# Latent attention layer: keys two heads at a time, queries split into rotary and plain tiles, caches laid out by the host

## The chip, the core and the metric

The kernel runs on one core of a Trainium2 chip. The metric is the device time of one execution in microseconds (us). The engines are named as in the profile: PE is TensorE, DVE is VectorE, ACT is ScalarE, POOL is GpSimd, SP is SyncE, which only issues the loads of the weights.

## What is computed

One step of a four-layer streaming encoder with a model width of 1024, for 256 frames of a new stream and 64 frames of a running stream. The kernel carries both as T = 320 columns. Layers 0 and 3 mix tokens by sparse attention, layer 1 by a recurrence, layer 2 by latent attention; each is followed by a gated feed-forward part. Only layer 2's mixer is touched. It is, cut to what matters:

```python
cq, ckv, kpe = jnp.split(h @ w_in, [512, 768], axis=-1)
q = (_rmsnorm(cq, g_q) @ w_uq).reshape(Bn, T, 16, 64 + 32)
q_nope, q_pe = q[..., :64], _rope(q[..., 64:], pos, 32)
lat, kpe = _rmsnorm(ckv, g_kv), _rope(kpe, pos, 32)
lat_all = jnp.concatenate([past_lat, lat], axis=1)      # 128 past + new rows, rank 256
kpe_all = jnp.concatenate([past_rope, kpe], axis=1)     # 32 columns, shared by the 16 heads
kv = (lat_all @ w_ukv).reshape(Bn, L, 16, 64 + 64)
k_nope, v = kv[..., :64], kv[..., 64:]
logits = (einsum('bthd,bshd->bhts', q_nope, k_nope) + einsum('bthr,bsr->bhts', q_pe, kpe_all)) * 96 ** -0.5
prob = softmax(where(chunk mask, logits, -inf))
return einsum('bhts,bshd->bthd', prob, v) @ w_out, lat, kpe
```

The new latents and rotary keys (`lat`, `kpe`) are outputs too.

## The kernel before

Every weight goes through the same pipeline. SP loads a slab of a weight matrix (up to 2304 columns per partition) into `raw`, ACT rounds it into `hi`, DVE writes the remainder `raw - hi` into `lo`, and PE makes three matmuls for each 128 rows of contraction (hi by x-hi, hi by x-lo, lo by x-hi, lines 919 to 921 in `product`). There are two buffers of each, so slab n takes the buffers of slab n-2: its `hi` waits until PE is done with that one. Each engine runs its own program, written out by hand, and the engines meet at counting semaphores; the order of the work on an engine is the order of its code.

Activations lie transposed, features on partitions and the 320 tokens (or 448 keys, 128 of the past and 320 new) along the columns. Layer 2's mixer (`pe_mla`, `act_mla`, `dve_mla`, `pool_mla`) has these stages.

1. Seven tiles of the input product (`for t in range(7)`): two tiles of `ckv`, one with the rotary key, four of `cq`. DVE evacuates them. The rotary key's tile is taken with its 32 rows at the end of 128, so PE moves them to rows 64 to 96 by two constant matrices (lines 1530 and 1531). The past latents and rotary keys come in by two loads on POOL's queue as rows, and PE turns them (three transposes, line 931); DVE copies them to `LATF` and, 16 times over, to `KC[64:96]` (lines 2645 and 2647).
2. For each half j of `w_ukv`: four value products into `VC` (lines 1550 to 1552), then eight key products, one for each head. A head's weights are 128 columns, 64 of the key and 64 of the value, and a key product takes all 128, of which ACT evacuates the first 64 rows into `KC[0:64]`. Behind the third value product `rows_turn` turns the new latents and rotary key into rows (nine transposes), ACT copies them to `lato` and `ropeo`, and POOL stores them by six DMAs.
3. The queries: `project(h)` makes head h's 96 rows (64 plain, 32 rotary), ACT evacuates them into `qraw`, DVE swaps the rotary halves (`swap`), and POOL makes three operations on 96 rows (`rope`, lines 691, 697, 699) that end in `QT`. Heads 0 to 7 are projected ahead of the loop, the other eight in it.
4. The loop over eight pairs of heads: PE makes the scores of pair p+2 (`pair_qk`), turns the probabilities of pair p, makes the first of two products, the values of pair p, and the second product. `maxima` and `probs` are on DVE, `exps` on ACT, the copies of the turned probabilities on both.

`tile_evac` counts evacuated tiles; PE writes a bank again when the tile two places back is evacuated. A product of the next stage waits for the last evacuation too.

## Time and profile before

| | us |
|---|---|
| median of 3 runs | 1736.91 |
| the three runs | 1736.82, 1736.91, 1745.93 |
| profiled execution, span from the first to the last instruction | 1731.7 |
| PE busy in the span | 1654.9 (96%) |
| DVE, ACT, POOL busy | 1143.0, 858.8, 749.0 |
| layer 2's mixer on PE, from its first product to its last pair | about 955 to 1093 |

For the profiled execution the profile gives the span and no time of its own beside it; the span is 5.2 us under the median of the runs. Matmuls overlap in the pipeline, so the time of a product is read from start to start, not from the durations. A timeline merges equal neighbours into one row with a count; the bracket names the idle time before the row and what ended it.

### The profile page before, as it was taken

The numbers are of one execution on the slowest core, as the hardware profiler recorded it, in microseconds if no ns is written. First come the engines' busy times: TensorE is split into PE (matmuls) and PEld (weight loads), VectorE is DVE, ScalarE is ACT, GpSimd is POOL, SyncE is SP. The second block draws the span as 40 slices with busy tenths as digits, with TensorE's granted clock in tenths as the row PEclk, the third lists the DMA queues.
The fourth block names the chain that finished last, engine by engine and source line by source line (L and its number), as shares of the span: only waits on it lengthen the run. The fifth ranks groups of instructions, "written<-read, shape, count | busy, mean of one in ns | idle before, by whom it ended". The sixth has DMA issues, their size and how long they took to land.

```text
span 1731.7 us, 37517 instructions
## 1 busy us (share of the span) xinstructions
PE 1654.9 (96%) x14117; PEld 1571.4 (91%) x14117; DVE 1143.0 (66%) x2046; ACT 858.8 (50%) x1622; POOL 749.0 (43%) x815
## 2 busy tenths in 40 slices
PE   7989999998988997999999999999999999999998
PEld 6869999996778997999999887999999977999997
DVE  4686777636477455677764738677774587777753
ACT  4474655524653433366643446366543356566533
POOL 5663666300044210366621446266631765466600
PEclk9999999999999999999999999999999999999999
DMA  7314556453230002455545412355545621555443
GB/s 207 94 51 138 154 145 161 128 153 108 84 113 17 10 4 82 126 154 153 143 134 156 122 51 74 108 159 146 145 133 149 165 85 58 149 153 152 123 140 112
DMA packets 344994, 205.11 MB, mean 118 GB/s; under 512 B 22456, under 2 KB 342312, under 8 KB 344752
## 3 DMA queue, kind: packets, MB, share of 16 engines
q1 hardware_dynamic: 342416, 198.97, 40.1%
q0 software_dynamic: 2080, 3.67, 0.7%
q8 instruction: 78, 1.28, 0.3%
q10 hardware_dynamic: 384, 0.88, 0.2%
q14 instruction: 36, 0.29, 0.1%
HBM read 200.02 MB, written 3.39 MB: 117 GB/s over the span
## 4 chain that ended last, share of the span: by engine, by line
PE 83%; DVE 7%; ACT 3%; issue 3%; POOL 2%; SPq 1%; DMA 1%; DVEq 0%; ACTq 0%; POOLq 0%
PE bank L919 23%; PE bank L920 23%; PE bank L921 23%; PE bank L1331 5%; PE bank L931 1%; ACT hi L1624 1%; DVE lo L2155 1%; SPq L564 1%; DVE SW L2354 1%; PE bank L1242 1%; PE bank L1355 1%; DVE top L2351 1%; PE bank L981 1%; PE bank L1270 1%; POOL qcos L691 1%
## 5 line engine op out<-in xcount | busy, mean ns | idle before, releaser
L919 PE MATMUL bank<-XH,hi 128*128 128x320 f32 (+1 forms) x1976 | 622.7, 315 | 9.1 <-DVE XL L2418 2.7
L2155 DVE TENSOR_TENSOR lo<-raw,hi 128x2048 fp32r<-128x2048 f32 (+2 forms) x196 | 418.0, 2133 | 299.4 <-ACT hi L1624 299.4
L920 PE MATMUL bank<-XL,hi 128*128 128x320 f32 (+1 forms) x1976 | 613.5, 310 | 0.0
L921 PE MATMUL bank<-XH,lo 128*128 128x320 f32 (+1 forms) x1976 | 613.2, 310 | 0.0
L1624 ACT ACTIVATE hi<-raw 128x2048 fp32r<-128x2048 f32 (+2 forms) x204 | 357.8, 1754 | 77.4 <-PE bank L921 61.7
L919 PEld LDWEIGHTS bank<-XH,hi 128*128 128x128 f32 (+1 forms) x1976 | 372.2, 188 | 22.8 <-issue 9.4
L920 PEld LDWEIGHTS bank<-XL,hi 128*128 128x128 f32 (+1 forms) x1976 | 372.3, 188 | 1.6 <-issue 0.4
L921 PEld LDWEIGHTS bank<-XH,lo 128*128 128x128 f32 (+1 forms) x1976 | 371.9, 188 | 0.0
L721 POOL TENSOR_TENSOR upad<-upad,rstd 128x128 f32<-128x128 f32 (+1 forms) x176 | 168.4, 976 | 199.2 <-ACT upad L1724 199.2
L919 PE MATMUL bank<-GH,hi 128*128 128x322 f32 x704 | 220.0, 313 | 1.8 <-DVE lo L2155 1.8
L920 PE MATMUL bank<-GL,hi 128*128 128x322 f32 x704 | 218.7, 311 | 0.0
L921 PE MATMUL bank<-GH,lo 128*128 128x322 f32 x704 | 218.0, 310 | 0.0
L726 POOL COPY ust<-upad 128x4 f32 (+1 forms) x176 | 210.0, 1223 | 14.4 <-POOL upad L721 13.9
L666 POOL TENSOR_TENSOR ssq<-ssq,sq 128x320 f32<-128x320 f32 x66 | 78.2, 1185 | 296.1 <-ACT sq L1772 223.9
L2266 DVE SCALAR_TENSOR_TENSOR conv<-upad,V,conv 128x322 f32<-128x322 f32 x352 | 171.0, 549 | 0.0
L1723 ACT COPY upad<-bank 128x64 f32<-128x64 f32 x176 | 39.2, 223 | 233.0 <-PE bank L921 233.0
L919 PEld LDWEIGHTS bank<-GH,hi 128*128 128x128 f32 x704 | 132.7, 188 | 2.4 <-DVE lo L2155 2.3
L920 PEld LDWEIGHTS bank<-GL,hi 128*128 128x128 f32 x704 | 133.1, 189 | 0.0
L921 PEld LDWEIGHTS bank<-GH,lo 128*128 128x128 f32 x704 | 132.4, 188 | 0.0
L1734 ACT ACTIVATE conv<-upad,V 128x322 f32<-128x322 f32 x176 | 106.3, 652 | 7.8 <-POOL upad L721 3.9
L1772 ACT ACTIVATE sq<-xT 128x320 f32<-128x320 f32 (+1 forms) x32 | 15.1, 472 | 132.0 <-DVE xT L2290 132.0
L1724 ACT COPY upad<-bank 128x256 f32<-128x256 f32 x176 | 68.0, 393 | 0.0
(388 smaller groups left out, 2375.0 us busy)
## 6 DMA issues: line engine op xcount, KB each, us to landing
raw<-in_f_w_up SPq DMA_DIRECT2D x176, 512.0 KB, 5.0
raw<-in_f_w_down SPq DMA_DIRECT2D x64, 704.0 KB, 4.7
raw<-in_a_w_in SPq DMA_DIRECT2D x12, 1024.0 KB, 5.4
raw<-in_b_w_rkv SPq DMA_DIRECT2D x12, 1024.0 KB, 5.2
raw<-in_a_w_out SPq DMA_DIRECT2D x8, 1024.0 KB, 5.2
raw<-in_b_w_out SPq DMA_DIRECT2D x4, 1024.0 KB, 5.1
raw<-in_c_w_out SPq DMA_DIRECT2D x4, 1024.0 KB, 5.2
raw<-in_a_w_in SPq DMA_DIRECT2D x12, 256.0 KB, 5.5
```

Of the source, the lines that this page charges most:

```text
L666: pool.tensor_tensor(ssq[:, :], ssq[:, :], sq[:, (c - 1) % 2, :], ALU.add).then_inc(ssq_done, 1)
L721: ins = pool.tensor_tensor(upad[:, j, :, cols_], upad[:, j, :, cols_], rstd[:, c:c + n_].rearrange("p (o n) -> p o n", o=1).to_broadcast([ ...
L726: ins = pool.tensor_copy(ust[:, seg, :, :].rearrange("p r (h f) -> p h r f", h=2)[:, :, :, bass.ds(f, 1)].rearrange("p h r f -> p h (r f)" ...
L919: pe.matmul(out, a, xh(k), start=(start and k == 0), stop=False)
L920: pe.matmul(out, a, xl(k), start=False, stop=False)
L921: last = pe.matmul(out, b, xh(k), start=False, stop=(stop and k == kt - 1))
L1331: last = pe.matmul(out[r_, col(q)], lhs[r_, q, :], rhs[r_, q, :], start=opens and (closes or q == 0), stop=closes, skip_group_check=True)
L1624: act.activation(hi[n % 2][:, 0:w_], raw[n % 2][:, 0:w_], ACT.Copy).then_inc(w_hi, 1)
L1724: ins = act.copy(upad[:, j, h, 68:TG + 2], ps[h][:, 64:T])
L1734: ins = act.activation(conv[:, j, h, :], upad[:, j, h, 2:TG + 2], ACT.Identity, scale=V[:, bass.ds(f + (w_ + NF * h), 1)], bias=V[:, bass. ...
L2155: dve.tensor_tensor(lo[n % 2][:, 0:w_], raw[n % 2][:, 0:w_], hi[n % 2][:, 0:w_].bitcast(F32), ALU.subtract).then_inc(w_lo, 1)
L2266: dve.scalar_tensor_tensor(out=conv[:, j, h, :], in0=upad[:, j, h, tap:tap + TG], scalar=V[:, bass.ds(f + (w_ + NF * h), 1)], in1=conv[:, ...
```

## The change

The host lays out four inputs differently and turns two outputs. The columns of `w_ukv` come as 512 of keys (eight heads) and 512 of values in each half, so that one key product covers two heads: eight key products in place of 16, and two ACT copies of 64 rows for each, for which the second moves rows 64 to 128 of the bank to rows 0 to 64 (`pair_evac`). The columns of `w_uq` come as 512 rotary ones (four tiles of 128 rows, four heads each) and then 1024 plain ones (eight tiles, two heads each): 12 products in place of 16, in three slabs of 2048 columns in place of four of 1536. The rotary work is one multiplication by the cosine and one by the sine on 128 rows for four heads, and one addition on 32 rows for each head, straight into `QT[64:96]`. ACT evacuates the plain tiles into `QT[0:64]`. Four rotary and two plain tiles come ahead of the first scores; in the loop a pair has one product, half of it before the values and half behind them. The past latents and rotary keys are loaded in place (the latter 16 times over, 256 KB), and the new ones are stored as they lie, by two DMAs, so that the moves by PE, the turns, and their copies go. The constants lose 192 columns. With one slab less, each later slab lies in the other buffer.

```diff
             for j in range(2):
-                slabs.append(Slab("ukv", j, 2, 1024, [(0, cols(i_["c_w_ukv"][inst], 1024 * j, 1024))], 12))
-            for j in range(4):
-                slabs.append(Slab("uq", j, 4, 384, [(0, cols(i_["c_w_uq"][inst], 384 * j, 384))], 4))
+                slabs.append(Slab("ukv", j, 2, 1024, [(0, cols(i_["c_w_ukv"][inst], 1024 * j, 1024))], 8))
+            for j in range(3):
+                slabs.append(Slab("uq", j, 4, 512, [(0, cols(i_["c_w_uq"][inst], 512 * j, 512))], 4))
...
-                chain(pool.memset(cr[:, :], 0.0))
-                pool.dma_start(cl[:, :], i_["cache_c_latent"][0, 0]).then_inc(cache_in, 16)
-                pool.dma_start(cr[:, 64:96], i_["cache_c_rope"][0, 0]).then_inc(cache_in, 16)
+                pool.dma_start(LATF[:, :, 0:PAST], i_["cache_c_latent"].rearrange("(k p) n -> p k n", p=128)).then_inc(cache_in, 16)
+                pool.dma_start(KC[64:96, :, 0:PAST], i_["cache_c_rope"]).then_inc(cache_in, 16)
...
                 pool.wait_ge(kc_rope, 1)
-                for z, (c, n_) in enumerate(TILES):
-                    pool.wait_ge(rows_out, ROWS_BEFORE[layer] + z + 1)
-                    for name, src in (("c_lat", lato[0:n_, z, :]), ("c_rope", ropeo[0:n_, z, 64:96])):
-                        store(o_[name + "_sample"][0, 0] if z == 0 else o_[name + "_prompt"][0, 0, 128 * (z - 1):128 * z], src)
+                store(o_["c_rope"], KPE[64:96, :])
+                pool.wait_ge(latf_done, 2)
+                store(o_["c_lat"].rearrange("(k p) n -> p k n", p=128), LATF[:, :, PAST:KEYS])
                 STORES_AT["latent"] = stores[0]
-                for h in range(16):
-                    if h >= 4:
-                        pool.wait_ge(qk_done, Q + h // 2 - 1)
-                    rope(Rb + 1 + h, E + 31 + h + 1, C("cos_c", 96), C("sin_c", 96), QT[0:96, (h // 2) % 2, h % 2, :], 96)
+                for i in range(4):
+                    r = Rb + 1 + i
+                    pool.wait_ge(tile_evac, E + 23 + i + 1)
+                    pool.tensor_tensor(QC[:, i, :], qraw[:, r % 2, :], C("cos_c"), ALU.mult).then_inc(cos_done, 1)
+                    pool.wait_ge(swap_done, r + 1)
+                    pool.tensor_tensor(QS[:, i, :], QS[:, i, :], C("sin_c"), ALU.mult).then_inc(rope_done, 1)
+                    pool.wait_ge(rope_done, r + 1)
+                    for h in range(4 * i, 4 * i + 4):
+                        if h >= 4:
+                            pool.wait_ge(qk_done, Q + h // 2 - 1)
+                        at_ = slice(32 * (h % 4), 32 * (h % 4) + 32)
+                        pool.tensor_tensor(QT[64:96, (h // 2) % 2, h % 2, :], QC[at_, i, :], QS[at_, i, :], ALU.add).then_inc(head_roped, 1)
...
                         pe.wait_ge(tile_evac, E + t - 1)
-                    product(psum[0 if t % 2 == 0 else 2][:, 0:T], n, (0, 128, 160)[t] if t < 3 else 128 * ((t - 3) % 2),
-                            lambda k: XH[:, k, :], lambda k: XL[:, k, :], before=x_ready(jn) if t == 0 else None)
+                    b, m = psum[0 if t % 2 == 0 else 2], 96 if t == 2 else 128
+                    product(b[0:m, 0:T], n, (0, 128, 192)[t] if t < 3 else 128 * ((t - 3) % 2),
+                            lambda k: XH[:, k, :], lambda k: XL[:, k, :], m=m, before=x_ready(jn) if t == 0 else None)
                     if t == 0:
                         mean_square(jn)
                     if t == 3:
-                        pe.wait_ge(tile_evac, E + 3)
-                        kpe = qraw[:, Rb % 2, :]
...
                         pe.wait_ge(rms_done, jn + 1)
...
-                            vh, vl = (w[:, k, :].rearrange("p (h c) -> p h c", c=128)[:, :, 64:128] for w in (wh, wl))
+                            vh, vl = (w[:, k, 512:1024] for w in (wh, wl))
...
                         if j == 0 and st == 2:
-                            rows_turn()
-                            pe.wait_ge(rows_out, ROWS_BEFORE[layer] + 1)
+                            pe.wait_ge(rms_done, norm_of[layer, "ckv"] + 1)
                             mean_square(norm_of[layer, "cq"])
-                    for h in range(8):
-                        e_ = 11 + 12 * j + h
+                    for g in range(4):
+                        e_ = 11 + 8 * j + g
...
-                        product(psum[0 if e_ % 2 == 0 else 2][:, 0:KEYS], n, 128 * h, lambda k: LATH[:, k, :], lambda k: LATL[:, k, :])
...
-                    product(psum[h % 2][0:96, 0:T], n, 96 * (h % 4), lambda k: XH[:, k, :], lambda k: XL[:, k, :], m=96)
-
-                for h in range(4):
-                    project(h)
+                        product(psum[0 if e_ % 2 == 0 else 2][:, 0:KEYS], n, 128 * g, lambda k: LATH[:, k, :], lambda k: LATL[:, k, :])
+
+                def project(u, first=0, end=None):
...
+                for u in range(6):
+                    project(u)
...
                 def pair_qk(p):
-                    pe.wait_ge(rope_done, Rb + 1 + 2 * p + 2)
+                    pe.wait_ge(tile_evac, E + 27 + p + 1)
+                    pe.wait_ge(head_roped, 2 * p + 2)
...
                 pair_qk(0)
-                project(4)
-                project(5)
+                project(6)
                 pair_qk(1)
-                project(6)
                 project(7)
...
                     if p + 4 < PAIRS:
-                        project(2 * p + 8)
+                        project(p + 8, 0, 2)
...
                     if p + 4 < PAIRS:
-                        project(2 * p + 9)
+                        project(p + 8, 2)
...
+                def pair_evac(e_, b, dst0, dst1, cols_):
+                    act.wait_ge(mm_done, done + e_ + 1)
+                    act.copy(dst0, psum[b][0:64, 0:cols_])
+                    act.copy(dst1, psum[b][64:128, 0:cols_]).then_inc(tile_evac, 1)
...
+                    for g in range(4):
+                        e_, h = 11 + 8 * j + g, 8 * j + 2 * g
+                        pair_evac(e_, 0 if e_ % 2 == 0 else 2, KC[0:64, h, :], KC[0:64, h + 1, :], KEYS)
+
+                def rope_tile(i):
+                    r = Rb + 1 + i
                     act.wait_ge(swap_done, r - 1)
                     act.wait_ge(cos_done, r - 1)
-                    evac(31 + h, qraw[0:96, r % 2, :], 96, T, h % 2)
-
...
+                rope_tile(0)
                 split_hi(s0 + 6)
-                for h in range(1, 4):
-                    head(h)
+                for i in range(1, 4):
+                    rope_tile(i)
                 split_hi(s0 + 7)
-                head(4)
-                head(5)
+                nope_tile(0)
+                nope_tile(1)
                 exps(Q)
-                head(6)
-                head(7)
+                nope_tile(2)
                 exps(Q + 1)
+                nope_tile(3)
                 for p in range(PAIRS):
                     pt_copy(Q + p)
                     if p + 2 < PAIRS:
                         exps(Q + p + 2)
                     out_hi(Q + p, p)
                     if p + 4 < PAIRS:
-                        head(2 * p + 8)
-                        if p in (0, 2):
-                            split_hi(s0 + 8 + p // 2)
-                        head(2 * p + 9)
+                        nope_tile(p + 4)
+                    if p == 0:
+                        split_hi(s0 + 8)
                     if p == 4:
-                        split_hi(s0 + 10)
+                        split_hi(s0 + 9)
                 mixer_out(layer, 1)
...
                     if t == 3:
                         split_lo(s0 + 2)
-                        dve.wait_ge(mla_turned, 1)
-                        dve.tensor_copy(LATF[:, :, 0:PAST], psum[6][:, 0:256].rearrange("p (k n) -> p k n", k=2))
-                        crt = psum[6][64:96, 256:384].rearrange("p (o n) -> p o n", o=1).to_broadcast([32, 16, PAST])
-                        dve.tensor_copy(KC[64:96, :, 0:PAST], crt).then_inc(mla_cached, 1)
+                        swap(Rb, E + 3, SWAP_C, 96)
...
+                def rope_tile(i):
+                    r = Rb + 1 + i
+                    dve.wait_ge(tile_evac, E + 23 + i + 1)
+                    dve.stream_shuffle(QS[:, i, :], qraw[:, r % 2, :], SWAP_C).then_inc(swap_done, 1)
...
+                    rope_tile(i)
+                split_lo(s0 + 7)
                 masks = [C("off0"), C("off1"), C("off0"), C("off1"), C("zero")]
                 maxima(Q, masks, C_SCALE)
-                head(4)
-                head(5)
                 maxima(Q + 1, masks, C_SCALE)
-                split_lo(s0 + 7)
...
-                    if p in (1, 3, 5):
-                        split_lo(s0 + 8 + p // 2)
+                    if p in (1, 5):
+                        split_lo(s0 + 8 + p // 4)
```

The order of POOL's instructions behind the copy of the rotary keys (`KC<-KPE`). `qcos`, `qsin`, `QC` and `QS` are rotary products, `QT` the queries that the scores read. Before:

```order
L811 COPY KC<-KPE 32x16x320 [waits rope_done,ssq_done]
L648 DMA out_c_lat_sample<-lato 64x256 [waits rows_out,kc_rope]
L648 DMA out_c_rope_sample<-ropeo 64x32
L648 DMA out_c_lat_prompt<-lato 128x256 [waits rows_out]
L648 DMA out_c_rope_prompt<-ropeo 128x32
L648 DMA out_c_lat_prompt<-lato 128x256 [waits rows_out]
L648 DMA out_c_rope_prompt<-ropeo 128x32
L691 TENSOR_TENSOR qcos<-qraw,con 96x320 [waits rope_done,tile_evac]
L697 TENSOR_TENSOR qsin<-qsin,con 96x320 [waits swap_done]
L699 TENSOR_TENSOR QT<-qcos,qsin 96x320 [waits cos_done,pool_c]
L691 TENSOR_TENSOR qcos<-qraw,con 96x320 [waits rope_done,tile_evac]
```

With the change:

```order
L794 COPY KC<-KPE 32x16x320 [waits rope_done,ssq_done]
L633 DMA out_c_rope<-KPE 32x320 [waits kc_rope]
L633 DMA out_c_lat<-LATF 128x2x320 [waits latf_done]
L803 TENSOR_TENSOR QC<-qraw,con 128x320 [waits tile_evac]
L805 TENSOR_TENSOR QS<-QS,con 128x320 [waits swap_done]
L811 TENSOR_TENSOR QT<-QC,QS 32x320 [waits rope_done]
L811 TENSOR_TENSOR QT<-QC,QS 32x320 [waits head_roped] x3
L803 TENSOR_TENSOR QC<-qraw,con 128x320 [waits tile_evac,head_roped]
L805 TENSOR_TENSOR QS<-QS,con 128x320 [waits swap_done]
L811 TENSOR_TENSOR QT<-QC,QS 32x320 [waits qk_done,rope_done]
L811 TENSOR_TENSOR QT<-QC,QS 32x320 [waits qk_done,head_roped] x3
L803 TENSOR_TENSOR QC<-qraw,con 128x320 [waits tile_evac,head_roped]
```

The six stores are two, and the three operations of a head are two operations for four heads and an addition for each, so the second cosine product stands behind four additions; with the second tile the additions wait for scores.

The order on ACT from the evacuation of the first half's key products on. `qraw` holds an evacuated rotary tile, `hi` is a weight slab's rounded part. Before:

```order
L2075 COPY KC<-bank 64x448 [waits mm_done] x8
L1624 ACTIVATE hi_55<-raw_53 128x1536 [waits mm_done,w_raw1]
L2075 COPY VC<-bank 128x512 [waits mm_done] x4
L2075 COPY KC<-bank 64x448 [waits mm_done] x8
L2075 COPY qraw<-bank 96x320 [waits mm_done,cos_done,swap_done]
L1624 ACTIVATE hi_54<-raw_52 128x1536 [waits mm_done,w_raw0]
L2075 COPY qraw<-bank 96x320 [waits mm_done,cos_done,swap_done] x3
L1624 ACTIVATE hi_55<-raw_53 128x1536 [waits mm_done,w_raw1]
L2075 COPY qraw<-bank 96x320 [waits mm_done,cos_done,swap_done] x2
```

With the change, from the last key evacuation on:

```order
L2063 COPY KC<-bank 64x448 [waits mm_done]
L2064 COPY KC<-bank 64x448
L2047 COPY qraw<-bank 128x320 [waits mm_done,cos_done,swap_done]
L1596 ACTIVATE hi_54<-raw_52 128x2048 [waits mm_done,w_raw0]
L2047 COPY qraw<-bank 128x320 [waits mm_done,cos_done,swap_done] x3
L1596 ACTIVATE hi_55<-raw_53 128x2048 [waits mm_done,w_raw1]
L2063 COPY QT<-bank 64x320 [waits mm_done]
L2064 COPY QT<-bank 64x320
L2063 COPY QT<-bank 64x320 [waits mm_done]
L2064 COPY QT<-bank 64x320
L1648 ACT_TABLE_LOAD
L1648 ACTIVATE LS_82,sums<-LS_82,negmax 128x128 [waits max_done]
```

The split of the third query slab still stands behind the fourth query tile, and the evacuation of the first plain tile, which the first scores need, now stands behind that split.

## Rows read from the trace of the kernel before

**Rows 1.** The page: busy time of the engines, and the chain that ended last by engine
```profile
PE 1654.9 (96%) x14117; PEld 1571.4 (91%) x14117; DVE 1143.0 (66%) x2046; ACT 858.8 (50%) x1622; POOL 749.0 (43%) x815
...
PE 83%; DVE 7%; ACT 3%; issue 3%; POOL 2%; SPq 1%; DMA 1%; DVEq 0%; ACTq 0%; POOLq 0%
```

**Rows 2.** Timeline of PE in layer 2 (start, duration, line, operation, count)
```profile
970.09 0.70 PE L1530 MATMUL bank<-qraw,con 128*96 128x320 f32 x2
...
971.49 0.70 PE L935 MATMUL bank<-ssq,con 128*128 128x320 f32 x2
...
988.47 0.38 PE L931 MATMUL bank<-con,LATF 128*64 128x128 f32 x2
...
989.71 0.81 PE L935 MATMUL bank<-ssq,con 128*128 128x320 f32 x2 [0.16 <-ACT ropeo L2096]
...
991.74 0.37 PE L919 MATMUL bank<-LATH,hi 128*128 128x448 f32 x1
...
1001.52 0.40 PE L1550 MATMUL bank<-hi,LATH 128*128 128x512 f32 x1
...
1007.11 0.36 PE L919 MATMUL bank<-LATH,hi 128*128 128x448 f32 x1
...
1017.71 0.36 PE L919 MATMUL bank<-XH,hi 128*96 128x320 f32 x1 [0.66 <-issue]
...
1019.53 0.30 PE L919 MATMUL bank<-XH,hi 128*96 128x320 f32 x1
...
1021.28 0.31 PE L919 MATMUL bank<-XH,hi 128*96 128x320 f32 x1
```

**Rows 3.** Timeline of ACT, the splits and evacuations around the key products
```profile
966.83 1.92 ACT L1624 ACTIVATE hi<-raw 128x2048 fp32r<-128x2048 f32 x1 [3.00 <-PE bank L921]
...
1001.72 0.53 ACT L2075 COPY KC<-bank 64x448 f32<-64x448 f32 x1 [0.69 <-PE bank L921]
1002.15 1.49 ACT L1624 ACTIVATE hi<-raw 128x1536 fp32r<-128x1536 f32 x1
...
1019.80 0.42 ACT L2075 COPY qraw<-bank 96x320 f32<-96x320 f32 x1 [2.19 <-PE bank L921]
```

**Rows 4.** Timeline of POOL: the key copy, and the first head's rotary work
```profile
985.86 4.45 POOL L811 COPY KC<-KPE 32x5120 f32<-32x5120 f32 x1
...
1020.30 0.87 POOL L691 TENSOR_TENSOR qcos<-qraw,con 96x320 f32<-96x320 f32 x1 [26.41 <-ACT qraw L2075]
1021.15 0.86 POOL L697 TENSOR_TENSOR qsin<-qsin,con 96x320 f32<-96x320 f32 x1
1022.09 2.28 POOL L699 TENSOR_TENSOR QT<-qcos,qsin 96x320 f32<-96x320 f32 x1
```

**Rows 5.** Timeline of DVE: weight splits of 2048 and 1536 columns, a PT copy
```profile
981.46 2.28 DVE L2155 TENSOR_TENSOR lo<-raw,hi 128x2048 fp32r<-128x2048 f32 x1
...
1021.64 1.99 DVE L2155 TENSOR_TENSOR lo<-raw,hi 128x1536 fp32r<-128x1536 f32 x1 [0.86 <-ACT hi L1624]
...
1050.01 0.69 DVE L2220 COPY PT<-bank 128x512 f32<-128x512 f32 x1
```

**Rows 6.** Timeline of PE in the loop over head pairs: scores (L951), turns (L931), values (L981)
```profile
1027.01 0.71 PE L951 MATMUL bank<-KC,QT 96*128 96x128 f32 x4 [2.05 <-POOL QT L699]
...
1038.84 0.71 PE L951 MATMUL bank<-KC,QT 96*128 96x128 f32 x4 [0.61 <-POOL QT L699]
...
1046.62 0.61 PE L951 MATMUL bank<-KC,QT 96*128 96x128 f32 x4
...
1048.50 1.09 PE L931 MATMUL bank<-con,LS 128*128 128x128 f32 x8
...
1069.64 0.61 PE L951 MATMUL bank<-KC,QT 96*128 96x128 f32 x4
...
1073.99 0.65 PE L981 MATMUL bank<-PT,VC 128*64 128x256 f32 x4 [1.37 <-ACT PT L1685]
...
1076.20 0.71 PE L951 MATMUL bank<-KC,QT 96*128 96x128 f32 x4 [0.97 <-POOL QT L699]
```

141 lines of the change are left out of this document (51 added, 90 removed).

## The prediction

> **What bounds the kernel now.** I read the page first: PE is busy for 96% of the span, and PE holds 83% of the chain that ended last [rows 1]. So a matmul taken away is worth its start-to-start time wherever PE had no wait, and a wait of PE's is worth what the other engines give back. The rest was read inside layer 2's mixer alone, on five timelines. PE's [rows 2]: the key products follow one another without a gap, eight in 991.74 to 1001.52, 1.22 us each; the four value products of a half take 1001.52 to 1007.11, 1.40 each; a query product takes 1.75 (1019.53 to 1021.28); and 0.66 idle stands at the seam between keys and queries. ACT's [rows 3]: what it splits and evacuates between products. POOL's and DVE's [rows 4, 5]: the rotary work and the splits that stand beside it. PE's in the loop [rows 6]: a pair takes 7.67 us ((1069.64 - 1046.62) / 3), and of the idle time there POOL's `QT` ends three pieces, 2.05, 0.61 and 0.97.
>
> **The sum, part by part.**
>
> The moves and turns. The two constant matrices and three turns take PE from 970.09 to 971.49, **1.40** [rows 2]. The nine turns and the wait for their copies take 988.47 to 989.71, **1.24**. Both go. PE then idles for DVE before the value products; that chain on DVE hangs on the evacuation of PE's fifth tile, so it comes earlier with it, and the idle time stays. The DVE copies that go lie ahead of that evacuation and give nothing more. ACT's six row copies and four of POOL's eight DMA issues go too and lay beside PE: nothing.
>
> The keys. Eight of 16 key products go, 8 x 1.22 = **9.78**, where PE never waited. ACT still makes 16 copies of 448 columns at 0.53 [rows 3]; two of them come to about 1.02 in a product of 1.22, so they stay covered. The price of a copy that moves rows 64 to 128 down by 64 isn't in the trace: between half of 0.53 (it would be cheaper only if the two overlapped) and twice that. I take 0.53, the same operation on as many rows. Twice would put 0.3 on each of eight products, 2.4.
>
> The seam inside the keys. The next slab's `hi` stands on ACT behind the last key copy and ahead of the first value evacuation. It grows from 1.49 (1536 columns) to 1.92 (2048), and a second copy of 0.49 stands before it [rows 3]. Counting from the first value product: copies end at 1.1, `hi` at 2.9, the first value evacuation at 3.45; the third value product wants that bank at 2.8. It waits **0.65**, where before it didn't. The seam to the queries waits for the last evacuation; a pair is 0.49 longer: **0.49** back.
>
> The queries ahead of the loop. Here the change adds waits. Let P be the start of the first query product. Before, P is 1017.71, the first scores start at P + 9.3 (1027.01) and the third at P + 21.1 (1038.84) [rows 2, 6]. Now: the first tile's evacuation runs from P + 2.1 to 2.5 [rows 3], POOL's cosine to 3.5 and sine to 4.3 (0.87 and 0.86, [rows 4]). ACT's split of the next slab (1.92) ends at 4.3 and DVE's `lo` of 2048 columns starts there, 2.28 us [rows 5]. Beside such a split POOL's operation took 2.28 in place of 0.86, and it ended 0.74 after DVE's did (1024.37 against 1023.63) [rows 4, 5]: POOL stands until DVE's operation is over. So the first addition ends at 7.45. The three others, 0.94 from start to start with their own waits (1021.15 to 1022.09), end at 10.3, and only then comes the second tile's cosine, to 11.1. ACT may not evacuate the fourth tile before it: 11.6. Then the split, 13.5, then the first plain tile's two copies, 14.2; PE's sixth product waits for the fourth evacuation and the first scores for the plain tile: P + 14.2. With two products and two scores (1.88 and a little) between, the third scores start at P + 21.8. PE does as many products up to there as before, eight of 1.75. **0.7** is lost.
>
> By the Trainium skill ("SBUF — State Buffer", section "SBUF: two separate sides") a VectorE operation with two SBUF inputs and a GpSimd operation lock each other out for the whole instruction. By that rule a row's longer time is a wait and not a slower rate; if it were only the 1.42 us that the row was longer by, the front would come out 0.8 better, and the sum 16.8.
>
> The price of a 32-row addition that reads one quarter of the partitions and writes another is not in the trace. Below, the key copy gives 4.45 / 16 = 0.28 for 320 columns on 32 rows; above, that whole copy, 4.45 [rows 4]. I take 0.86, the nearest row: the same operation, one third of whose rows it is.
>
> The loop. Counting from the scores' start: turns begin at 1.88 (1048.50) and end at 2.7; half a product, 0.9, ends at 3.6. DVE's copy of the turned probabilities starts at 3.39 and takes 0.69 [rows 5, 6], and with no full product to hide it the values start at about 4.3, as they do at 1073.99 with 4.35. So 0.7 us of waiting, hidden before behind the second half of a full product, shows in each pair. Values 1.2 and the other half 0.9 end at 6.4. Pair 0 (7.78 before) gives 1.38; pairs 1 to 3 give 1.27 each, less 0.7 for one, in which DVE's 2048-column `lo` pushes the maxima out; pair 4 (1069.64 to 1076.20, 6.56) comes to 5.6 as POOL's 0.97 goes: 1.38 + 3.81 - 0.7 + 0.96 = **5.45**, of the 7.0 that four products are worth. From pair 5 on both programs are alike.
>
> Covered: the load of the past rotary keys, 256 KB in place of 16, is issued as the layer begins and is wanted by DVE's cast behind the fifth tile, several products later. If that cover were gone it would cost the transfer. Fewer constants and the other buffer parity: nothing, since every later slab does the same work.
>
> Sum: 1.40 + 1.24 + 9.78 + 5.45 - 0.65 - 0.49 - 0.70 = **16.0 us**. The profiled span goes from 1731.7 to 1715.7. The median of the runs lies 5.2 over the span; carried along, it goes from 1736.9 to **1720.9**.
>
> By "TensorE: Matmul & The Clock Gate" of the Trainium skill, section "Back-to-back issue gap", an isolated matmul of N columns takes N/2.4 + 2.5 ns, 189 for 448 columns, where rows 2 show 1.22 / 6 = 204. With it the key term would be 9.1 and not 9.78; the measured spacing decides.
>
> **Rivals.** A measurement of this kernel can tell about 0.5%, 8.7 us, from no change.
>
> All of it comes through. PE gives 1.40 + 1.24 + 9.78 + 7.0 = 19.4, and the three waits for POOL (3.63) go as well: 23, so 1714. For it: POOL has 24 operations where it had 48. Against it: the loop's wait for DVE and ACT [rows 6] is a chain that doesn't shrink with PE's work, and POOL's four additions in a row stand before the second cosine. Chance 0.14.
>
> The loop gives nothing: if the exponentials, the normalisation and the copies already set 7.67 per pair, the products only filled it, and the gain is 16.0 - 5.45 = 10.6, so 1726.3. Against it: the rows of PE at the start of pairs 1 and 4 name no idle time [rows 6], and pair 4, which has no product, took 6.56, of which 0.97 was a wait for POOL. Chance 0.1.
>
> The change does much less than it says: the loop gives nothing and the copies that move rows, or the additions, cost half again as much (2.4 for the copies), which leaves 16.0 - 5.45 - 2.4 = 8.1: 1728.8, about 1729. Chance 0.07.
>
> Slower: the 32-row additions are slow because they move rows to another quarter of the partitions. At 4.45 each (the upper bound) the first scores wait 4 x 3.5 = 14 us longer, at P + 28, and the 12 additions and three pairs of products behind them (12 x 4.45 + 5.2 = 58.6) bring the last scores to P + 87, against 58.5 before (1076.20 - 1017.71). Since P itself comes 11.3 earlier, that is 17 us slower: 1754. It decides from 3.3 us an addition on (with a for the addition the last scores start at P + 17.6 + 16a, and 58.5 + 11.3 = 69.8), four times the row I take; below 2.3 the loop doesn't feel it. Against it: POOL's copy moves 5120 columns on 32 rows in 4.45. Chance 0.04.
>
> **How the numbers follow.** My forecast has 0.65. Its own range is 1717 to 1724: below, the three small losses (0.65, 0.49, 0.7) don't show, and the front gains as POOL stands beside no split; above, the copies cost 2.4 more. Faster by over 0.5%: 0.65 + 0.14 + 0.1 = 0.89; within: 0.07; slower: 0.04. The range 1714 to 1727 takes in the two rivals on its ends and leaves out 0.11 and the tails.
>
> **What would show it.** Four key products 1.22 apart in each half of the weights, and a gap of about 0.65 at the third value product of the second half. The fourth rotary tile's evacuation ended by POOL's second cosine; the first scores about 14 us behind the first query product. In the loop 6.4 from scores to scores, with PE waiting for the copies of `PT` in each pair. POOL's additions near 0.86. Wrong would be an addition over 2 us, a pair still at 7.6, or the value products waiting for the caches.

## The result, and the profile after

| | before | the changed kernel |
|---|---|---|
| median of the runs made side by side, us | 1736.87 | 1720.3 (1718.74 to 1723.49, 4 runs) |
| ratio of the times | | 0.9904, 95% interval 0.9879 to 0.993 |
| span of the profiled execution | 1731.7 | 1718.6 (its own time 1720.39) |
| layer 2's mixer on PE, first input product to the last pair's values | 136.33 | 122.41 |

The kernel got faster, by 16.6 us; 1720.9 was forecast, in a range of 1714 to 1727. What can be read without noise is the mixer itself: it lost **13.9** us, where 16.0 were forecast. So the forecast of the median came out better than its working, and that is luck: 5.2 us lay between the span and the median before, 1.8 between the span and the time of the changed kernel's profiled execution, and that difference filled up what the layer fell short by. The spans lie 13.1 us apart, where 16.0 were forecast as well.

The page of the changed kernel, busy time and the chain, against [rows 1]:

```profile
PE 1637.5 (95%) x14005; PEld 1555.8 (91%) x14005; DVE 1134.6 (66%) x2021; ACT 859.5 (50%) x1618; POOL 725.3 (42%) x786
...
PE 81%; DVE 7%; issue 3%; ACT 3%; POOL 3%; SPq 1%; DMA 1%; DVEq 0%; ACTq 0%; POOLq 0%
```

PE has 112 matmul instructions less. Its busy time fell by 17.4 us and the span by 13.1, so PE idles 4.3 us more than before. It is still the bound, with a slightly smaller share of the chain.

PE's timeline in the changed kernel, where the stages begin ([rows 2] are those of before). L910 is the first matmul of a product, L1523 that of a value product:

```profile
989.52 0.36 PE L910 MATMUL bank<-LATH,hi 128*128 128x448 f32 x1
...
992.07 0.47 PE L910 MATMUL bank<-LATH,hi 128*128 128x448 f32 x1
...
994.80 0.47 PE L1523 MATMUL bank<-hi,LATH 128*128 128x512 f32 x1
...
998.38 0.50 PE L1523 MATMUL bank<-hi,LATH 128*128 128x512 f32 x1 [0.58 <-ACT VC L2047]
...
1001.24 0.36 PE L910 MATMUL bank<-LATH,hi 128*128 128x448 f32 x1
...
1007.69 0.38 PE L910 MATMUL bank<-XH,hi 128*128 128x320 f32 x1 [1.20 <-issue]
...
1019.50 0.38 PE L910 MATMUL bank<-XH,hi 128*128 128x320 f32 x1 [2.79 <-ACT qraw L2047]
```

The four key products of a half take 994.80 - 989.52 = 5.28, where four of 1.22 would be 4.88. The third value product of the second half waits, as forecast, and the queries begin (P) at 1007.69. Then comes the place to look at: the sixth query product waits 2.79 for the evacuation of the fourth rotary tile.

ACT's timeline shows why the key products are no longer free of waits, against [rows 3] (L2063 and L2064 are the two copies of a key tile):

```profile
990.94 0.53 ACT L2063 COPY KC<-bank 64x448 f32<-64x448 f32 x1 [0.64 <-PE bank L912]
991.48 0.53 ACT L2064 COPY KC<-bank 64x448 f32<-64x448 f32 x1
...
995.79 1.92 ACT L1596 ACTIVATE hi<-raw 128x2048 fp32r<-128x2048 f32 x1
...
1018.93 0.43 ACT L2047 COPY qraw<-bank 128x320 f32<-128x320 f32 x1 [5.20 <-POOL QC L803]
1019.30 1.92 ACT L1596 ACTIVATE hi<-raw 128x2048 fp32r<-128x2048 f32 x1
1021.12 0.40 ACT L2063 COPY QT<-bank 64x320 f32<-64x320 f32 x1
1021.53 0.42 ACT L2064 COPY QT<-bank 64x320 f32<-64x320 f32 x1
```

A copy that moves rows costs the same 0.53 as one that doesn't. But there are two banks, and the third product needs that of the first: a product (1.22), 0.2 until ACT starts, two copies (1.07) and 0.06 until PE starts make 2.55 (989.52 to 992.07), and two products only 2.44. The fourth tile's evacuation waited for POOL's second cosine (`QC`), and ACT's split and the plain tile's copies stand behind it.

POOL's and DVE's timelines of the same stretch, against [rows 4, 5]. On POOL, L803 multiplies by the cosine, L805 by the sine, and L811 adds, one head at a time. On DVE, L2126 makes `lo` and L2184 normalises the probabilities of a pair:

```profile
1010.30 0.87 POOL L803 TENSOR_TENSOR QC<-qraw,con 128x320 f32<-128x320 f32 x1 [19.10 <-ACT qraw L2047]
1011.14 0.87 POOL L805 TENSOR_TENSOR QS<-QS,con 128x320 f32<-128x320 f32 x1
1012.10 5.82 POOL L811 TENSOR_TENSOR QT<-QC,QS 32x320 f32<-32x320 f32 x4
1018.00 0.86 POOL L803 TENSOR_TENSOR QC<-qraw,con 128x320 f32<-128x320 f32 x1
```

```profile
1012.06 2.29 DVE L2126 TENSOR_TENSOR lo<-raw,hi 128x2048 fp32r<-128x2048 f32 x1 [1.28 <-ACT hi L1596]
...
1030.24 3.26 DVE L2184 TENSOR_SCALAR LS<-LS,rsum 128x128 f32<-128x128 f32 x5
...
1035.62 1.24 DVE L2184 TENSOR_SCALAR LS<-LS,rsum 128x128 f32<-128x128 f32 x5
```

Four additions took 5.82: the first 3.0 while DVE's `lo` ran, the others 0.87, as the view of POOL's instructions that write `QT` gives them (least, median and longest in ns):

```profile
L811 POOL TENSOR_TENSOR QT<-QC,QS x4: 853/870/2995, 1012.1 to 1017.1; 32x320 f32<-32x320 f32 x4
```

On 32 rows, read from one quarter of the partitions and written to another, an addition takes the time of one on 96 rows (0.87 in the median of the 16 additions of before).

PE's timeline in the loop, against [rows 6]: scores at L942, turns at L922, values at L972.

```profile
1022.53 0.97 PE L942 MATMUL bank<-KC,QT 96*128 96x128 f32 x4
...
1030.37 0.61 PE L942 MATMUL bank<-KC,QT 96*128 96x128 f32 x4
...
1033.56 1.09 PE L922 MATMUL bank<-con,LS 128*128 128x128 f32 x8 [1.24 <-DVE LS L2184]
...
1037.75 0.61 PE L942 MATMUL bank<-KC,QT 96*128 96x128 f32 x4
...
1040.48 0.39 PE L910 MATMUL bank<-XH,hi 128*128 128x320 f32 x1
...
1041.93 0.65 PE L972 MATMUL bank<-PT,VC 128*64 128x256 f32 x4 [0.33 <-issue]
...
1043.11 0.42 PE L910 MATMUL bank<-XH,hi 128*128 128x320 f32 x1
...
1044.09 0.61 PE L942 MATMUL bank<-KC,QT 96*128 96x128 f32 x4
```

From scores to scores the pairs take 7.38 (1030.37 to 1037.75), 6.34 (1037.75 to 1044.09), then 7.04, 6.34 and 5.35. From the half product ahead of the values (1040.48) to the values PE takes 1.45, from the half behind them (1043.11) to the next scores 0.98: the values wait 0.47. POOL's `QT`, which ended three waits before, ends none here.

What the granted clock was while PE took up work again (columns: stretch, then its length, then busy time with instruction count for PE, PE's weight loads, DVE, ACT and POOL, then the granted clock, the DMA share and GB/s):

```profile
1018.00:1019.50 1.50, 0.00 (x0) 0.03 (x1) 0.10 (x2) 0.57 (x2) 1.50 (x2) 1.00 0.52 180
1019.50:1021.00 1.50, 1.50 (x7) 1.50 (x8) 0.41 (x1) 1.50 (x1) 0.17 (x1) 0.62 0.07 16
1021.00:1022.50 1.50, 1.50 (x7) 1.50 (x6) 1.25 (x1) 0.94 (x3) 0.00 (x0) 0.50 0.00 0
```

After 2.79 us of idle time the granted clock fell from 1.00 to 0.50, from 2.4 to 1.2 GHz. The sixth product, 12 matmuls, took 3.03 (1019.50 to 1022.53) instead of 1.75. Before, PE waited 2.05 near this place [rows 6], and the clock stayed at 1.00.

### The profile page after: what moved, and what is told of

It is laid out like the page before. It is cut to its first block, busy times and chain, and to the rows that moved or that the text cites. A ratio compares the mean times of both kernels' runs of the same rounds, so it can differ in the third digit from the quotient of the medians.

```text
span 1718.6 us, 37190 instructions
## 1 busy us (share of the span) xinstructions
PE 1637.5 (95%) x14005; PEld 1555.8 (91%) x14005; DVE 1134.6 (66%) x2021; ACT 859.5 (50%) x1618; POOL 725.3 (42%) x786
## 3 DMA queue, kind: packets, MB, share of 16 engines
q8 instruction: 77, 1.26, 0.3%
## 4 chain that ended last, share of the span: by engine, by line
PE 81%; DVE 7%; issue 3%; ACT 3%; POOL 3%; SPq 1%; DMA 1%; DVEq 0%; ACTq 0%; POOLq 0%
PE bank L910 23%; PE bank L911 22%; PE bank L912 22%; PE bank L1322 5%; ACT hi L1596 1%; PE bank L922 1%; DVE lo L2126 1%; PE bank L1233 1%; DVE SW L2325 1%; SPq L549 1%; PE bank L972 1%; PE bank L1346 1%; DVE top L2322 1%; POOL qcos L676 1%; PE bank L1330 1%
## 5 line engine op out<-in xcount | busy, mean ns | idle before, releaser
L910 PE MATMUL bank<-XH,hi 128*128 128x320 f32 x1960 | 618.3, 315 | 12.5 <-ACT qraw L2047 2.8
L2126 DVE TENSOR_TENSOR lo<-raw,hi 128x2048 fp32r<-128x2048 f32 (+1 forms) x195 | 418.4, 2146 | 293.4 <-ACT hi L1596 293.4
L912 PE MATMUL bank<-XH,lo 128*128 128x320 f32 x1960 | 609.1, 311 | 0.0
L911 PE MATMUL bank<-XL,hi 128*128 128x320 f32 x1960 | 609.0, 311 | 0.0
L1596 ACT ACTIVATE hi<-raw 128x2048 fp32r<-128x2048 f32 (+1 forms) x203 | 357.6, 1762 | 77.0 <-PE bank L912 61.7
L910 PEld LDWEIGHTS bank<-XH,hi 128*128 128x128 f32 x1960 | 370.9, 189 | 26.3 <-issue 13.0
L911 PEld LDWEIGHTS bank<-XL,hi 128*128 128x128 f32 x1960 | 371.2, 189 | 1.5 <-issue 0.2
L912 PEld LDWEIGHTS bank<-XH,lo 128*128 128x128 f32 x1960 | 370.8, 189 | 0.0
L910 PE MATMUL bank<-GH,hi 128*128 128x322 f32 x704 | 220.0, 312 | 1.8 <-DVE lo L2126 1.8
L711 POOL COPY ust<-upad 128x4 f32 (+1 forms) x176 | 209.9, 1223 | 14.4 <-POOL upad L706 13.9
L910 PEld LDWEIGHTS bank<-GH,hi 128*128 128x128 f32 x704 | 132.7, 188 | 2.3 <-DVE lo L2126 2.3
```

The costliest lines, as they stand in the source:

```text
L711: ins = pool.tensor_copy(ust[:, seg, :, :].rearrange("p r (h f) -> p h r f", h=2)[:, :, :, bass.ds(f, 1)].rearrange("p h r f -> p h (r f)" ...
L910: pe.matmul(out, a, xh(k), start=(start and k == 0), stop=False)
L911: pe.matmul(out, a, xl(k), start=False, stop=False)
L912: last = pe.matmul(out, b, xh(k), start=False, stop=(stop and k == kt - 1))
L1596: act.activation(hi[n % 2][:, 0:w_], raw[n % 2][:, 0:w_], ACT.Copy).then_inc(w_hi, 1)
L2126: dve.tensor_tensor(lo[n % 2][:, 0:w_], raw[n % 2][:, 0:w_], hi[n % 2][:, 0:w_].bitcast(F32), ALU.subtract).then_inc(w_lo, 1)
```

## The experiments

Every run was read in the same way, by the starts of PE's rows in layer 2. The layer is counted from the start of the first input product to the start of the last pair's values; P is the start of the first query product. turns_back, keys_twice, loop_twice, lo_waits, seam and front_both ran once each. The time outside the layer, the span less the layer, lies between 1595.4 and 1605.5 us in these profiled executions and goes in part with the granted clock of other layers (in 1300 to 1400 us it is 1.00 in some and 0.95 in others); the layer repeats within 0.1 (the rows changed and again). So the verdict on a mechanism is the layer's, and the medians only say what it is worth in all.

| kernel | to P | first scores | third scores | pair 0's turns | from scores to scores | layer |
|---|---|---|---|---|---|---|
| before | 62.73 | P+9.30 | P+21.13 | P+23.12 | 7.78 7.67 7.68 7.67 6.56 | 136.33 |
| changed | 52.17 | P+14.84 | P+22.68 | P+25.87 | 7.38 6.34 7.04 6.34 5.35 | 122.41 |
| again | 52.12 | P+14.79 | P+22.69 | P+25.88 | 7.39 6.33 7.04 6.34 5.35 | 122.36 |
| turns_back | 54.49 | P+14.31 | P+21.91 | P+25.10 | 7.39 6.34 7.04 6.34 5.36 | 123.97 |
| keys_twice | 61.38 | P+14.32 | P+24.53 | P+27.72 | 7.38 6.34 7.04 6.34 5.35 | 133.47 |
| loop_twice | 52.12 | P+15.04 | P+22.68 | P+25.88 | 9.02 7.71 7.69 7.69 5.36 | 127.36 |
| lo_waits | 52.15 | P+16.72 | P+24.20 | P+27.41 | 7.40 6.34 7.02 6.34 5.36 | 123.92 |
| seam | 51.73 | P+14.78 | P+22.70 | P+25.90 | 7.39 6.34 7.03 6.34 5.36 | 122.00 |
| whole_ahead | 52.13 | P+15.04 | P+22.66 | P+25.86 | 7.16 5.93 6.57 5.94 5.46 | 120.96 |
| cos_first | 52.14 | P+10.63 | P+19.65 | P+22.02 | 6.56 6.34 6.79 6.34 5.36 | 118.28 |
| front_both | 52.15 | P+10.63 | P+19.81 | P+21.77 | 6.52 6.34 6.79 6.34 5.36 | 118.41 |
| all_four | 51.82 | P+10.63 | P+19.80 | P+21.76 | 5.92 5.93 6.54 5.93 5.46 | 116.50 |

**The changed kernel once more** (again), with nothing edited.

> The changed kernel once more, for its distance from the kernel before. The stages of its profile give 13.9 us in the latent layer and 13.1 in the span. If the layer is all there is, the ratio comes near 0.992 (13.9 us less); if the first comparison's 16.6 us is real, something outside the layer gives 3 us more, and the stretches ahead of the layer or behind it are shorter than before in this profile too. I expect 14 to 15 us.

Measured: 1722.52 us (1720.41 to 1728.62) against 1739.77, a ratio of 0.9912 (0.9887 to 0.9936). The layer took 122.36. A gain of 13.9 us is a ratio of 0.992, and both intervals hold it. The medians lie 17.3 us apart, more than the 14 to 15 expected, but nothing outside the layer got shorter in this profile: 958.4 us lie ahead of it and 640.6 behind it, against 955.0 and 640.4 before.

**The moves and the turns put back** (turns_back). PE does the two constant matrices and the 12 turns again, into banks that nobody reads; the copies that followed them are not put back.

```diff
                     if t == 3:
+                        pe.wait_ge(tile_evac, E + 3)
+                        kpe = qraw[0:96, Rb % 2, :]
+                        pe.matmul(psum[3][0:96, 0:T], C("ones", 96)[:, 0:96], kpe, start=True, stop=True)
+                        pe.matmul(psum[1][0:96, 0:T], C("ones", 96)[:, 0:96], kpe, start=True, stop=True)
+                        pe.wait_ge(cache_in, 16 * CACHE_LOADS[layer])
+                        for k in range(2):
+                            turn(psum[6][:, 128 * k:128 * k + 128], LATF[:, k, 0:128])
+                        turn(psum[6][:, 256:384], LATF[:, 0, 0:128])
                         pe.wait_ge(rms_done, jn + 1)
...
+                            pe.wait_ge(latf_done, 2)
+                            pe.wait_ge(rope_done, Rb + 1)
+                            for z, (c, n_) in enumerate(TILES):
+                                b_ = psum[(7, 6, 4)[z]]
+                                for k in range(2):
+                                    turn(b_[0:n_, 128 * k:128 * k + 128], LATF[:, k, PAST + c:PAST + c + n_])
+                                turn(b_[0:n_, 256:352], KPE[:, c:c + n_])
                             mean_square(norm_of[layer, "cq"])
```

> PE makes two products of 96 rows and three transposes behind the fourth input tile and nine transposes behind the third value product, into banks that nobody reads, as the kernel before did with use. It measures the two terms of the moves and turns. Theory: the value products start 1.4 us later and the key products 1.1 us beyond that; 2.5 in all. Rival (they lay in PE's wait for DVE, and the value products start when DVE is ready): the first 1.4 don't show.

Measured: P comes 2.32 later (2.5 expected), 1.40 from the moves and 0.92 from the nine turns, behind which no copies stand here. The layer is 123.97. PE's rows:

```profile
972.78 0.70 PE L1511 MATMUL bank<-qraw,con 96*96 96x320 f32 x2
...
974.19 0.70 PE L926 MATMUL bank<-ssq,con 128*128 128x320 f32 x2
...
1024.01 0.39 PE L910 MATMUL bank<-XH,hi 128*128 128x320 f32 x1 [2.78 <-ACT qraw L2062]
1026.51 0.71 PE L942 MATMUL bank<-KC,QT 96*128 96x128 f32 x4 [0.51 <-ACT QT L2079]
```

This run shows something else by chance. The same wait of 2.78 stands ahead of the sixth query product, and this time the clock stayed:

```profile
1024.00:1026.00 2.00, 1.99 (x12) 1.74 (x12) 0.67 (x2) 2.00 (x2) 0.18 (x1) 1.00 0.01 4
```

The scores then start at P + 14.31 and the third ones at P + 21.91; P + 14.2 and P + 21.8 were forecast. In the changed kernel they stand 0.53 and 0.77 later. So the fallen clock costs 0.77 of the layer there, if the turns, long done by then, change nothing else in the front; the rest of the front is what the prediction said.

**Every key product twice** (keys_twice): PE makes each one once more into the same bank, with nothing evacuated between; it only adds work.

```diff
+                        product(psum[0 if e_ % 2 == 0 else 2][:, 0:KEYS], n, 128 * g, lambda k: LATH[:, k, :], lambda k: LATL[:, k, :], end=2)
                         product(psum[0 if e_ % 2 == 0 else 2][:, 0:KEYS], n, 128 * g, lambda k: LATH[:, k, :], lambda k: LATL[:, k, :])
```

> Each of the eight key products is made twice, so PE does as many as before the change. It measures the key term of the sum. Theory (8 x 1.22 = 9.78, less what PE already waits for the pairs of copies, 0.4 a half): the first query product comes 9.0 us later, and the key products stand 1.22 us apart without waits. Rival (PE waits for ACT there, so that the halved products are worth much less than 9.78): under 6 us later.

Measured: P comes 9.21 later (9.0 expected), so eight key products are worth 9.2 where ACT's copies have room. The layer is 11.06 longer, and 1.85 of that is the clock again, which stood at 0.50 for 6 us here:

```profile
1032.00:1034.00 2.00, 1.85 (x8) 1.45 (x7) 1.71 (x1) 1.94 (x6) 0.00 (x0) 0.50 0.00 0
1034.00:1036.00 2.00, 2.00 (x8) 1.17 (x8) 0.58 (x1) 1.17 (x1) 0.00 (x0) 0.50 0.10 30
1036.00:1038.00 2.00, 2.00 (x9) 1.46 (x10) 1.14 (x9) 0.00 (x0) 0.95 (x2) 0.50 1.00 319
```

**A whole second query product in each pair** (loop_twice): in pairs 0 to 3 each half is made whole.

The second one is work that the result does without.

```diff
-                        project(p + 8, 0, 2)
+                        project(p + 8, 0, 4)
...
                     if p + 4 < PAIRS:
-                        project(p + 8, 2)
+                        project(p + 8)
```

> In the loop pairs 0 to 3 make their query product twice, once whole ahead of the values and once whole behind them, so PE has the products of the kernel before there. Theory (the loop gave 5 and not 7 us, since without the work PE waits for the copies of PT): pairs come back to 7.67 us, pair 0 to 7.8 to 8.4, together 3 to 4 us more than with the change. Rival (PE is the bound in the loop also after the change): 7.0 us more.

Measured: the layer is 4.95 longer, with pairs 1 to 3 back at 7.7, the 7.67 of before. Four products of 1.75 are 7.0; 2.05 of it went into idle time that is there with one product. That is the forecast's reading of the loop, seen from the other side. But 3 to 4 was expected, and pair 0 at 7.8 to 8.4; it took 9.02, since PE waits 1.25 for DVE ahead of its turns, as in the changed kernel, and the expectation didn't count that wait.

**DVE's split behind the first additions** (lo_waits). DVE makes the second tile's swap and waits until four heads are added before it makes `lo`.

```diff
                 rope_tile(0)
+                rope_tile(1)
+                dve.wait_ge(head_roped, 4)
                 split_lo(s0 + 6)
-                for i in range(1, 4):
+                for i in range(2, 4):
```

> DVE makes its 2048-column split (lo) of the second query slab only when the four additions of the first tile are done. Theory (an operation of POOL stands while such an operation of DVE runs): the first addition takes 0.87 instead of 3.0 us, the four end 2.1 us earlier, and the fourth query tile's evacuation starts about 2.1 us earlier, though PE's fifth product may now wait for the split, until about P + 10.5. Rival (the first addition is slow of itself, as the first of its kind or because it moves rows to other partitions): it stays near 3 us.

Measured: layer +1.51. POOL's timeline, and DVE's row of the moved split:

```profile
1011.87 3.71 POOL L811 TENSOR_TENSOR QT<-QC,QS 32x320 f32<-32x320 f32 x4
1015.65 2.97 POOL L803 TENSOR_TENSOR QC<-qraw,con 128x320 f32<-128x320 f32 x1
```

```profile
1015.61 2.29 DVE L2126 TENSOR_TENSOR lo<-raw,hi 128x2048 fp32r<-128x2048 f32 x1 [2.94 <-POOL QT L811]
```

Without the split beside them the four additions take 3.71 instead of 5.82; the cosine that now runs beside it takes 2.97 instead of 0.86. The 2.1 us go with DVE's operation, wherever it stands: a wait, not a price of the addition. So the second cosine ends no earlier, and the fourth evacuation starts at P + 11.25, where 2.1 us earlier than P + 11.24 was expected. And `lo` itself starts 3.8 later (P + 8.16 against P + 4.37), so PE's fifth product now waits for it:

```profile
1017.95 0.63 PE L910 MATMUL bank<-XH,hi 128*128 128x320 f32 x1 [3.23 <-DVE lo L2126]
```

The granted clock stood at 0.50 from 1017.45 to 1023.45 in this run, so the fifth and sixth products took 6.22 together (1017.95 to 1024.17), where two take 3.5 at 1.00. How much of the 1.51 is the later `lo` and how much the clock, this run doesn't tell.

**Cosines ahead of the additions** (cos_first). POOL does the next tile's cosine and sine before the additions of heads that are not yet wanted.

```diff
-                for i in range(4):
+                def rotary(i):
...
+                rotary(0)
+                rotary(1)
+                add(0)
+                add(1)
+                rotary(2)
+                add(2)
+                add(3)
+                rotary(3)
+                for h in range(4, 16):
+                    add(h)
```

> POOL makes the second tile's cosine and sine before the first head's addition, the third's before heads 2 and 3. Theory (the fourth evacuation waits for the second cosine, which stands behind four additions): PE's wait of 2.8 us before the sixth query product goes, the first scores start at P + 11 instead of P + 14.8, pair 0's turns at P + 21 instead of P + 25.9, and the kernel is about 5 us shorter. Rival (ACT's split and PE's own eight products set the front, POOL is only in step with them): the wait moves to another releaser and under 1.5 us are won.

Measured: 1720.64 us (1716.39 to 1723.43), ratio 0.989 (0.986 to 0.992); the layer is **4.13** shorter (about 5 expected). Timelines of ACT and of PE (in this kernel scores are at L955, turns at L935):

```profile
1015.82 0.43 ACT L2060 COPY qraw<-bank 128x320 f32<-128x320 f32 x1 [1.44 <-POOL QC L803]
1016.19 1.92 ACT L1609 ACTIVATE hi<-raw 128x2048 fp32r<-128x2048 f32 x1
```

```profile
1024.17 0.68 PE L955 MATMUL bank<-KC,QT 96*128 96x128 f32 x4 [1.26 <-issue]
...
1030.35 1.09 PE L935 MATMUL bank<-con,LS 128*128 128x128 f32 x8 [0.41 <-DVE LS L2197]
```

The fourth evacuation starts at P + 7.49 (P is 1008.33) instead of P + 11.24, PE doesn't wait ahead of the sixth product, the first scores come at P + 10.63 and the clock stays at 1.00. Of the 4.2 won there 3.0 are left at the third scores: PE waits 1.26 ahead of the second ones, whose additions now stand behind the third tile's cosine, and that took 2.80 beside DVE's `lo`:

```profile
1018.55 2.80 POOL L803 TENSOR_TENSOR QC<-qraw,con 128x320 f32<-128x320 f32 x1
```

Pair 0 gives another 0.8, as DVE's normalisation takes 2.43 here and not 3.26, and pair 2 gives 0.25. The medians don't show the gain: 1720.64 against 1722.52 for the changed kernel (again), with overlapping intervals.

**Plain tiles and the first maxima ahead of the split as well** (front_both).

```diff
-                split_hi(s0 + 7)
                 nope_tile(0)
                 nope_tile(1)
+                split_hi(s0 + 7)
...
-                split_lo(s0 + 7)
                 maxima(Q, masks, C_SCALE)
+                split_lo(s0 + 7)
```

> The reordered rotary work of the earlier run, and besides: ACT evacuates plain tiles 0 and 1 ahead of the split of the next slab, and DVE takes the first pair's maxima ahead of its `lo` of that slab. With the rotary work alone reordered the layer took 118.28 us, with the first scores at P + 10.63 and pair 0's turns at P + 22.02. If what is left in front is that split standing ahead of DVE's and ACT's work on pair 0 (PE waited 1.26 ahead of the first scores' second half and 0.41 ahead of the turns), the turns come at P + 20.5 to 21.5 and the layer takes 117.3 to 118.0. If the split only moves its place, as it did where DVE's split waited, the layer takes 118.3 or more. The span cannot tell this: its spread outside the layer is over 2 us.

Measured: layer 118.41, against 118.28 with the rotary work alone, so the second reading of the expectation holds. Pair 0's turns come 0.25 earlier, and that is gone again by the end. The split only moved: PE no longer waits ahead of the second scores, but ahead of the third:

```profile
1028.98 0.68 PE L955 MATMUL bank<-KC,QT 96*128 96x128 f32 x4 [1.54 <-POOL QT L813]
```

**Whole products** (whole_ahead): the product of a pair is made whole ahead of the values, with no half behind them.

```diff
-                        project(p + 8, 0, 2)
+                        project(p + 8)
...
-                    if p + 4 < PAIRS:
-                        project(p + 8, 2)
```

> In the loop the whole query product stands ahead of the values and nothing behind them. Theory (with half a product the values wait for DVE's and ACT's copies of the turned probabilities, a latency that PE can fill): a pair goes from 6.34 to about 5.8 us from scores to scores, 2 to 2.5 us less in all. Rival (the pair is set by the work of DVE and ACT on it, not by that latency): the pair stays at 6.3 and the idle time moves to the next scores or turns.

Measured: 1725.21 us (1719.45 to 1729.91), ratio 0.9907 (0.9875 to 0.9939). The medians show no gain over the changed kernel (1722.52, again); this kernel's profiled execution has 1605.4 outside the layer. The pairs take 5.93 instead of 6.34 (5.8 expected), and the layer is 1.45 shorter (2 to 2.5 expected). PE's rows of one pair:

```profile
1042.34 0.71 PE L942 MATMUL bank<-KC,QT 96*128 96x128 f32 x4
...
1044.32 1.09 PE L922 MATMUL bank<-con,LS 128*128 128x128 f32 x8
1045.17 0.39 PE L910 MATMUL bank<-XH,hi 128*128 128x320 f32 x1
...
1047.10 0.65 PE L972 MATMUL bank<-PT,VC 128*64 128x256 f32 x4
```

The whole product takes 1.93 up to the values (1045.17 to 1047.10), two halves 2.43 in the changed kernel (1.45 and 0.98): the wait for the copies of `PT`, 0.47, is gone whole. Only 0.4 shows, because the scores, now right behind the values, take 1.98 up to the turns instead of 1.88.

**The second half's split among the value evacuations** (seam): ACT makes `hi` of the next slab behind the second value evacuation, not ahead of the first.

```diff
-                    split_hi(s0 + 4 + j)
+                    if j == 0:
+                        split_hi(s0 + 4)
                     for st in range(4):
+                        if j == 1 and st == 2:
+                            split_hi(s0 + 5)
```

> ACT splits the first query slab behind the second value evacuation of the second half and not ahead of the first. Theory (the third value product waits for the first evacuation, which stands behind a split of 1.92 us): its wait of 0.58 us goes, and the time from the first value product to the first key product goes from 6.44 back to 5.6, 0.85 less. Rival (the wait only moves: the fourth value product or the first key product then waits for the evacuations behind the split): under 0.3 less.

Measured: P comes 0.44 earlier, half of what was expected. PE no longer waits ahead of the third value product, but the last evacuations now stand behind the split:

```profile
1001.20 0.47 PE L910 MATMUL bank<-LATH,hi 128*128 128x448 f32 x1 [0.25 <-ACT VC L2047]
```

**All of them** (all_four): the edits of cos_first, front_both, whole_ahead and seam.

> All the edits that gave something, together: rotary work reordered, plain tiles and the first maxima ahead of the split, whole query products at the same place in each pair, the second half's split between the key copies. Singly the layer got shorter by 4.1 (rotary work), 1.4 (whole products) and 0.4 (split), against 122.4 us. If they are separate waits they add up: layer 115.5 to 117, and the time 5 to 7 us under the changed kernel's, 1713 to 1717, about 1.3% under the kernel before. If they cure the same waits, the layer stays at 117.5 to 118.5.

Measured: 1718.4 us (1715.64 to 1721.41, 6 runs) against 1735.77, ratio 0.9894 (0.987 to 0.9919); the profiled span is 1713.8. The layer is 116.50 (115.5 to 117 expected), **5.9** under the changed kernel's and 19.8 under that of before, and the singles add up: 4.13 + 1.45 + 0.41 = 6.0. The time is a miss: 1713 to 1717 was expected, about 1.3% under the kernel before, and it is 1.1%. The medians alone would not show the gain over the changed kernel: the interval overlaps that one's (0.9887 to 0.9936). One wait of the front is left, the one of 1.5 that front_both has ahead of the third scores.

## Why the prediction was right, and where it wasn't

| step | forecast | measured in the layer |
|---|---|---|
| moves and constant matrices | 1.40 | 1.44 |
| turns | 1.24 | 1.32 |
| keys with their two seams | 9.78 - 0.65 - 0.49 = 8.64 | 7.80 |
| queries ahead of the loop, to the third scores | -0.70 | -1.55 |
| loop | 5.45 | 4.91 |
| sum | 16.0 | 13.9 |

- **Moves and turns.** Right, and shown by putting them back (1.40, and 0.92 for the nine turns without the wait for their copies). The covered loads were covered: nothing waited for the caches.
- **Keys.** "They stay covered" was wrong by a little. What counts is not ACT's share of a product (1.07 in 1.22) but the loop through two banks: 2.55 for two products of 2.44, and again at the seam, where the first value product wants the bank of the third key product. The first half gave 4.50 and not 4.88, the second 4.15 and not 4.39 with its seam, and the seam inside the keys cost 0.85 and not 0.65: 0.8 in all. That the products themselves are worth 9.2, keys_twice shows.
- **The front.** The chain was right link by link: the evacuation ended by POOL's second cosine, at P + 11.24 (11.2 forecast), the split at P + 11.6, the plain tile at P + 14.3. What failed is the unwritten step behind it, that PE does its products at the same clock after a wait of 2.8 us. The fall cost 0.77 here and 2.6 in keys_twice, measured against turns_back, where the clock stayed. In cos_first the wait is gone, and the clock stays at 1.00.
- **POOL standing for DVE's split.** Right: 3.0 for the first addition against 0.87 for the others, and the wait moves with the split. By the Trainium skill ("SBUF — State Buffer", section "SBUF: two separate sides") whichever of the two starts first has the shared port pair for its whole instruction; the trace agrees, since the addition ends 0.7 after `lo` (1015.1 against 1014.35) and the moved split made the next operation stand in the same way.
- **The loop.** Pairs 1 to 4 came about as forecast (6.4 with 0.7 for one of them and 5.6; measured 6.34, 7.04, 6.34, 5.35), with a wait of 0.47 for the copies of `PT` where 0.7 was counted. Pair 0 was to take 6.4 and took 7.38. PE waits 1.24 there for DVE's normalisation, five operations in 3.26 beside POOL's additions and cosine. The same five take 1.24 in pair 1, where POOL idles, and with POOL's work arranged otherwise (cos_first) 2.43, the pair then 6.56. That POOL's work is the cause is read from these three rows; no run changed it alone. The forecast counted DVE's copy as the last wait of a pair and had no row for this one.
- **From the span to the median.** The 5.2 that the forecast carried along was no property of the kernel. In the executions on record that give both, the span is 1.8 to 1.9 under the time, so the profiled execution before took about 1733.5 by this estimate and was one of the fast ones; 3.4 of the 5.2 are that. The layer fell 2.1 short of its sum, and the median hit by luck.
- **The rivals.** All comes through (23 us) fell because the loop keeps a wait in each pair. The loop gives nothing fell, as 4.9 of 7.0 came, and with it the one that gains 8.1; the copies that move rows cost no more than the others. Slower fell too: an addition takes 0.87. Its two sums in the forecast differ by 1.8 us (P + 87 in the one, 17.6 + 16 x 4.45 = 88.8 in the other), which moves its threshold from 3.3 to 3.4 and changes nothing else.

Still open: what decides whether the clock falls after a wait of 2.8 us.

## What to carry to other kernels

When one tile holds four heads, the engine behind it gets its work in larger lumps: four additions in a row ahead of the next cosine made PE wait 2.8 us, although POOL had half as many operations as before. Put what the next tile's evacuation waits for ahead of what only a later consumer wants; that alone was worth 4.1 us of the layer, three tenths of what the whole change gave. And whether copies are covered is decided by the loop through the buffers, not by one engine's share: here product, handover, both copies and handover, against two products.

## What the runs showed of the hardware that wasn't expected

- With the same idle time of 2.8 us ahead of the same product, the granted clock fell to 0.50 for some 3 us in five runs (the changed kernel, again, loop_twice, seam, whole_ahead), for 6 us in keys_twice, and not at all in turns_back. At 0.50 a matmul of 320 columns takes 0.265 from start to start instead of 0.146. By the Trainium skill ("TensorE: Matmul & The Clock Gate", section "Part 1: The HAM clock gate (the "warmup" mystery)") the clock gate passes either half of the pulses or all, which the rows agree with.
- An operation of POOL on two tiles of 320 columns takes 0.87 in the median whether it has 32 rows (the additions), 96 (the additions of before) or 128 (the cosine products). Fewer rows save nothing here; fewer operations do.
- An ACT copy takes 0.53 for 64 rows of 448 columns whether it leaves the rows in place or moves them down by 64.
